# Decoder layer with RWKV-7 heads: b and k are brought to the recurrence as rows of tokens

## What is computed

```python
def rwkv7_recurrence(r, w, k, v, a, b):
    def step(state, inp):
        r_t, w_t, k_t, v_t, a_t, b_t = inp
        sa = jnp.einsum('bhvk,bhk->bhv', state, a_t)
        state = (state * w_t[:, :, None, :] + sa[..., None] * b_t[:, :, None, :]
                 + v_t[..., None] * k_t[:, :, None, :])
        y_t = jnp.einsum('bhvk,bhk->bhv', state, r_t)
        return state, y_t
    ...
def rwkv7_group(u, ...):
    u = u + f(mu_shift) * (token_shift(u) - u)
    r, k, v, wl, al, gl = jnp.split(u, RWKV_SPLITS, axis=-1)
    ...
    y = rwkv7_recurrence(r_h, hs(decay), k_mod, v_h, -kk, kk * alpha_h)

def reference(x, ...):
    h = rms_norm(x, pre_mix_norm[layer])
    proj = (h @ w_in[layer]).astype(jnp.float32)
    y_rwkv = rwkv7_group(proj[..., :RWKV_COLS], ...)
    y_pool = multiscale_pool(proj[..., RWKV_COLS:], ...)
    mixed = jnp.concatenate([y_rwkv, y_pool], axis=-1) @ w_out[layer]
    x = x + rms_norm(mixed, post_mix_norm[layer])
    f = conv_ffn(rms_norm(x, pre_ffn_norm[layer]), w_up, conv_w, conv_b, w_down)
    x = x + rms_norm(f, post_ffn_norm[layer])
```

## Time and profile before

| | us |
|---|---|
| median of three runs | 2341.03 |
| lowest, highest | 2337.63, 2349.45 |
| the profiled execution's own time | 2339.92 |
| its span on the core | 2338.1 |
| project phase | 0 to 549 |
| recurrence | 549 to about 850 |
| busy TensorE, VectorE, ScalarE, GpSimd | 2232.0, 1760.7, 1142.7, 1016.1 |

### The profile page before, as it was taken

One profiled execution on the slowest core, in us unless ns is written; L12 is line 12 of the kernel. 1 busy time (PEld: TensorE's weight loads), 2 busy tenths in 40 slices (PEclk: granted clock), 3 DMA queues, 4 the chain that ended last, 5 costly groups with the idle time before them and its releaser, 6 DMA issues.

```text
span 2338.1 us, 43613 instructions
## 1 busy us (share of the span) xinstructions
PE 2232.0 (95%) x16652; PEld 1816.3 (78%) x16652; DVE 1760.7 (75%) x1905; ACT 1142.7 (49%) x1794; POOL 1016.1 (43%) x726
## 2 busy tenths in 40 slices
PE   7999999996989979998999999999999999999998
PEld 5787777775878758886888888788788888887886
DVE  2666798894785466768999998666799898986555
ACT  4656555452445554444444444454544444444543
POOL 4646465571233335534777767100146555541000
PEclk9999999998999989999999999999999999999999
DMA  7374556347567547886434343677743233326774
GB/s 197 96 234 128 191 148 208 105 143 211 150 171 190 143 135 235 268 279 177 148 110 151 108 149 122 218 248 250 245 129 115 93 111 105 112 94 209 239 259 145
DMA packets 435786, 395.60 MB, mean 169 GB/s; under 512 B 59516, under 2 KB 352044, under 8 KB 432300
## 3 DMA queue, kind: packets, MB, share of 16 engines
q1 hardware_dynamic: 407772, 343.06, 47.6%
q10 hardware_dynamic: 27856, 50.34, 6.0%
HBM read 266.97 MB, written 126.35 MB: 168 GB/s over the span
## 4 chain that ended last, share of the span: by engine, by line
PE 54%; DVE 3%; DMA 2%; ACT 1%; issue 1%; SPq 1%; POOL 0%; ACTq 0%; DVEq 0%; POOLq 0%
PE late_bank L133 18%; PE late_bank L135 18%; PE late_bank L134 18%; DVE wt_lo L2886 1%; DMA raw<-scratch_td 1%; ACT wt_hi L2707 1%; PE late_bank L2181 1%; DMA raw<-in_w_up 0%; DMA raw<-in_w_down 0%; DVE wt_lo L2840 0%; DMA p_keep<-in_w_down 0%; DMA p_keep<-scratch_td 0%; DVE conv_val L2867 0%; DVE p_ub L2849 0%; SPq L1966 0%
## 5 line engine op out<-in xcount | busy, mean ns | idle before, releaser
L133 PE MATMUL late_bank<-o_hi,wt_hi 128*128 128x512 f32 x1232 | 482.1, 391 | 9.6 <-DVE p_ub L2849 3.1
L134 PE MATMUL late_bank<-o_lo,wt_hi 128*128 128x512 f32 x1232 | 481.4, 391 | 0.0
L135 PE MATMUL late_bank<-o_hi,wt_lo 128*128 128x512 f32 x1232 | 481.2, 391 | 0.0
L426 POOL TENSOR_TENSOR p_w_lo<-p_w_raw,p_w_hi 128x1024 fp32r<-128x1024 f32 x72 | 190.4, 2645 | 217.3 <-ACT p_w_hi L494 217.3
L133 PEld LDWEIGHTS late_bank<-o_hi,wt_hi 128*128 128x128 f32 x1232 | 232.3, 189 | 60.9 <-issue 9.5
L135 PEld LDWEIGHTS late_bank<-o_hi,wt_lo 128*128 128x128 f32 x1232 | 232.5, 189 | 48.6
L134 PEld LDWEIGHTS late_bank<-o_lo,wt_hi 128*128 128x128 f32 x1232 | 232.3, 189 | 48.2
L2577 POOL TENSOR_TENSOR tsum<-raw 128x512 f32<-128x512 f32 x43 | 104.1, 2420 | 366.0 <-DVE p_ub L2927 180.7
L133 PE MATMUL p_ppr<-p_hT_hi,p_w_hi 128*128 128x512 f32 x576 | 233.3, 405 | 0.3 <-POOL p_w_lo L426 0.2
L133 PE MATMUL late_bank<-wt_hi 128*128 128x512 f32 x572 | 223.2, 390 | 7.7 <-ACT wt_hi L2707 6.0
L135 PE MATMUL p_ppr<-p_hT_hi,p_w_lo 128*128 128x512 f32 x576 | 226.5, 393 | 0.0
(11 more groups left out here) (327 smaller groups left out, 4669.2 us busy)
## 6 DMA issues: line engine op xcount, KB each, us to landing
raw<-in_w_up SPq DMA_DIRECT2D x88, 512.0 KB, 5.1
p_w_raw<-in_w_in SPq DMA_DIRECT2D x72, 512.0 KB, 3.9
scratch_a<-p_keep SPq DMA_DIRECT2D x22, 1280.0 KB, 4.5
raw<-scratch_a SPq DMA_DIRECT2D x96, 256.0 KB, 3.0
raw<-scratch_td SPq DMA_DIRECT2D x52, 256.0 KB, 3.5
p_keep<-scratch_a SPq DMA_DIRECT2D x47, 256.0 KB, 3.0
scratch_a<-p_keep SPq DMA_DIRECT2D x44, 256.0 KB, 2.0
raw<-in_w_down SPq DMA_DIRECT2D x44, 256.0 KB, 4.1
```

What stands on the lines that cost most here:

```text
L133: nc.tensor.matmul(out, lhs_hi, rhs_hi, start=start, stop=False, skip_group_check=again)
L134: nc.tensor.matmul(out, lhs_hi, rhs_lo, start=False, stop=False, skip_group_check=again)
L135: return nc.tensor.matmul(out, lhs_lo, rhs_hi, start=False, stop=stop, skip_group_check=again)
L426: nc.gpsimd.tensor_tensor(w_lo[i][:, :, :], w_raw[i][:, :, :], w_hi[i][:, :, :].bitcast(F32), ALU.subtract).then_inc(s_wl, 1)
```

## The change

In the project phase b and k are turned into rows like v and a: `turn_b` at pair 8 (in the last block ahead of its last tile), k of the block before at pair 1 (for the last block at the very end). ScalarE reads both (`b_rows` behind the last tile of a block, `k_rows` at f = 3 of the next) and stores them as "bT" and "kT", 1 MB each for a block, and several waits are moved to them. In the recurrence `bkt` has another layout and is zeroed once by GpSimd; SyncE loads its rows from "bT" and "kT", eight loads of 32 partitions x 2 x 256 for a superchunk (`load_rows`). The transposes of `bk` and ScalarE's reads of them go; GpSimd still builds `bk` for the Gram products. TensorE's order is another: `w_products` stand behind the first `from_state`, `z0_products` behind the second, the Gram products are spread over the last two chunks. ScalarE's reads of w move to the front.

The core of the diff:

```diff
@@ phase_project, scalar
+                def b_rows(b):
+                    act.wait_ge(s_btn, ONE + b + 1)
+                    act.wait_ge(s_vst, ONE + b * 16 + 16)
+                    read_rows(gate, [pm[:, g, :] for g in range(TT)], s_br)
+                    act.wait_ge(s_br, ONE + b + 1)
+                    store_rows("bT", b, gate[:, :, :], s_brst)
...
+                        if f == 3 and b > 0:
+                            k_rows(b - 1)
...
+                        if f == (FT - 1 if more else FT - 2):
+                            b_rows(b)
...
+                k_rows(BLOCKS - 1)
@@ phase_project, gpsimd
                     if f == K0:
                         gp.wait_ge(s_kst, ONE + b * 16)
+                        gp.wait_ge(s_ktn, ONE + b)
@@ phase_project, tensor
+                    if b < BLOCKS - 1:
+                        pe.wait_ge(s_br, ONE + b + 1)
                     for g in groups:
...
+                    if pair == 1 and b > 0:
+                        pe.wait_ge(s_ar, ONE + b)
+                        pe.wait_ge(s_kt, ONE + b)
+                        rows(um[:, K0:K0 + PAIRS, :], [pm[:, g, :] for g in range(TT)], s_ktn)
+                    if pair == 8 and b < BLOCKS - 1:
+                        turn_b(b)
...
+                            if b == BLOCKS - 1 and f == FT - 1:
+
+
+                                turn_b(b)
                             for k in range(KT):
+                                if b == BLOCKS - 1 and f == FT - 1 and k == 1:
+                                    pe.wait_ge(s_br, ONE + b + 1)
...
+                pe.wait_ge(s_pout, ONE + BLOCKS * 2)
+                pe.wait_ge(s_kt, ONE + BLOCKS)
+                rows(um[:, K0:K0 + PAIRS, :], [pm[:, g, :] for g in range(TT)], s_ktn)
@@ phase_recur, sync
+                def load_rows(n):
+                    if n < 2:
+                        sp.wait_ge(s_const, ONE + 3)
+                    else:
+                        sp.wait_ge(s_s, ONE + (n - 1) * CH)
+                    for e in range(2):
+                        for kind in range(2):
+                            for h in range(2):
+                                dst = bkt[n % 2][quad(kind, h), :, h, :, :].rearrange("s (c e) j v -> s e c (j v)", e=2)[:, e]
+                                sp.dma_start(dst, bkrow[(kind + e) % 2][n, e, h]).then_inc(s_rows[n % 2], 16)
...
+                    if a2 and i >= 0:
+                        load_rows(i + 1)
@@ phase_recur, gpsimd
-                        if b:
-                            wait_full(gp, i - 1, "bk3")
+                        if i >= 0:
+                            gp.wait_ge(s_gram, ONE + i + 1)
@@ phase_recur, tensor
+                        if c4 == 0:
+                            pe.wait_ge(s_rows[p], ONE + i // 2 * 128 + 128)
...
                     if a2:
-                        bk_transposes(0)
+                        w_products()
...
                     if a2:
-                        bk_transposes(1)
+                        z0_products()
                     if b:
                         to_state(1)
                     if o:
                         from_uv()
-                    if a2:
-                        bk_transposes(2)
                     if b:
                         from_state(2)
-                    if a2:
-                        bk_transposes(3)
+                    if o:
+                        from_r(1)
                     if b:
                         to_state(2)
-                    if o:
-                        from_r(1)
-                    if a2:
-                        z0_products()
+                    if a1:
+                        grams(0)
                     if b:
                         from_state(3)
                     if a1:
-                        grams(0)
+                        grams(1)
                     if b:
                         to_state(3)
-                    if a2:
-                        w_products()
                     if a1:
-                        for j in range(1, PAIRS):
+                        for j in range(2, PAIRS):
                             grams(j)
```

## The result

| | us |
|---|---|
| median of four runs after | 2380.6 |
| lowest, highest | 2377.5, 2381.7 |
| before, beside it (four runs) | 2340.4 |
| ratio after / before | 1.0163, 95% interval 1.0134 to 1.0192 |
| the profiled execution's own time, its span | 2380.6, 2378.8 |

Slower by 40 us, where 17 were forecast: the time lies above the range. In the two traces the recurrence's first load is issued at 549.3 before and at 571.3 after; the first `to_state` of body 15 lies at 822.3 and 860.9. So the project phase costs 22 us, as forecast, the recurrence up to body 15 another 16.5 us, where 4 were to be gained, and the rest some 2.

The account below looks back on a forecast made before the run. TensorE was taken to bound the project phase and SyncE's issue time to become the recurrence's bound. 2339.9 + 22 (project phase) - 4 (recurrence: 7 gained, 3 lost to couplings) = 2358 us, range 2335 to 2370.

Parts of the forecast that it names:

- Project phase, +22: Project phase: turning b and k adds 5.0 + 7.9 + 4.4 + 4.7 = 22 us, bounds 16 and 27.
- TensorE's body of 13.2 us: Recurrence: without the four transpose groups (2.4 us) TensorE alone could do a body in 13.2 us, from 15.35.
- The 0.2 us a body of new stalls in the chain: Recurrence: the new product order adds about 0.2 us of stalls between state products and updates, 13.0 becoming 13.2.
- A set of row loads, 4.6 us of SyncE: Recurrence: eight added 64 KB loads a body take 4.1 to 5.3 us of SyncE's issue time, 4.6 taken.
- SyncE as the bound: Recurrence: with the row loads SyncE needs 16.9 us a body, against the 13.2 that TensorE could do.
- All of SyncE's 53 us of waits can be used: Recurrence: 74 us of added issue fill SyncE's 53.1 us of waits, so its last loads end at 812, not 791.3.
- The couplings, 3 us: Recurrence: late inverse block and late bonus and gate loads together lose 3 us, cutting the gain from 7 to 4.
- the other coupling: Recurrence, body 4: the last inverse block's load comes some 8 us later, delaying VectorE's solving step before the first state update.
- Rival 3: Recurrence: TensorE's stalls lower its clock, 10 to 12 us longer, 2370; chance 0.12 with anything above 2366.
- My own sign for it: Recurrence: TensorE's clock falling under 0.9 between bodies 8 and 14 would show the forecast wrong the other way.
- Rival 1: Recurrence: the loads are hidden, bodies run at TensorE's or VectorE's pace, 30 us gained, 2332; chance 0.12.
- the 7 us gained at SyncE's pace: Recurrence: with all SyncE waits used, body 15 begins at 815 instead of 822.3, 7 us gained before the couplings.

## Why the prediction was wrong

- **Project phase, +22.** Right: 22.1 us in the trace of after, 22.5 in the run of this half alone. Its parts are less exact, and that they cancel is luck: the first dense product of the fourth block comes 14.3 us later than in before (415.67 for 401.40), where three seams and two turns of k gave 11.2; the fourth block adds 3.8 more up to its last dense product (552.94 for 534.86), for 6.1; and the end adds 4.0, for 4.7.
- **TensorE's body of 13.2 us.** Right as a lower bound (12.99 in body 8 of after), wrong as a pace: without row loads the bodies at full clock mostly take 14 to 15, and 7 of 15 run at a lower one. The 0.2 us a body of new stalls in the chain were too few: TensorE's waits for VectorE's updates grow by 14.4 us in sum there (7.0 to 21.4), and stops for instructions were not in the sum at all.
- **A set of row loads, 4.6 us of SyncE.** Right: 72.4 us for 128 loads, 4.5 a set. SyncE as the bound is right too: no loads, half of the loads and the shared loads show it.
- **All of SyncE's 53 us of waits can be used.** Wrong by 11: 11.4 us of waits remain, 4.9 of them for the place of a row set itself. The last gate load of bodies with loads, at 790.55 in the earlier trace rows, comes at 839.34, 26.7 us later beyond the project's 22.1, where 74 - 53 = 21 were reckoned.
- **The couplings, 3 us.** This is the step that failed. I had the chain (gate, GpSimd, mix store) and its 3.6 us of slack, but let only the second update wait behind it. I even wrote that TensorE stands there 2 to 4 us in most bodies, and then put 3 us for both couplings into the sum, as if SyncE's pace would hide the rest; no row showed that it would. It does not: bodies 4 to 13 of after take 18.8 us in the mean, where SyncE's pace was to be 16.9. The new order puts the w reads behind that same store, and `TURN` puts y into w0's bank, so that TensorE stands already at the y transposes, ahead of the second product with the state, for up to 7.8 us and 25.8 us in sum. Reordering did not cure it: with the w reads ahead the wait went to u, with gate ahead to VectorE and GpSimd. With SyncE's queue full something else was late in each order tried, and the price is paid in body after body, not once at the end. The late inverse block, the other coupling, came 11.5 us late instead of 8 (load at 666.44; 632.79 + 22.1 = 654.9 expected without the change), in the same body 4 in which gate was late too; the runs with one of the two moved show that either alone keeps that body at 24 us or more.
- **The start.** Not reckoned: the first `to_state` comes 5 us later than with the project half alone, behind eight more loads and the w products, which wait for inverse blocks. The one attempt to undo it failed, so how the 5 us divide is not shown.
- **Rival 3, the clock.** It is there: bodies 4 to 13 of after have a mean of 14.66 us of TensorE busy time at clocks down to 0.73, against 12.93 at full clock. It comes behind the waits and adds to them; I had it as a case of its own with 10 to 12 us, and did not join it to the forecast, although I forecast waits of 2 to 4 us in most bodies, and a stand of 2.5 us brought it on (body 12 above). My own sign for it, a clock under 0.9 between bodies 8 and 14, came true with 0.77 in body 9.
- **Rival 1, loads hidden.** Even with no loads its 2332 is not reached: 2361. The 26 us that the shorter TensorE body should give, had nothing else been late, were 5.
- **The terms, by the runs.** Project half +22.5; recurrence without row loads 5 less, +17.3; its row loads +22.9; together the +40.2 of after. So the project term and SyncE as the place of the loss were seen rightly; what the loads cost, and what the missing transposes give, were not.

In the forecast's own sum: +22 held; the 7 us gained at SyncE's pace shrink to 1 (26.7 for 21); and the couplings, with the start and the clock behind the waits, are the rest of the 16.5, some 18 us instead of 3; how much of it is couplings, start and clock each is known only as far as the bodies above tell.

## What to carry to other kernels

Before work is moved from a compute engine to loads, add up the issue time of the queue for each body, not its waits over the whole. When that sum nears the body's length, the last loads of the queue come late in body after body, and each costs as much as what waits for it; the orders tried here only moved the loss. Keep the added loads under the slack, or share them between two issuing queues; here four on each did what eight on one did not. And a gap that a removed product leaves between serial steps gives back only a part of its length: put the work back in a harmless form and see how much time it costs before counting on it. Where a matmul engine stops without a releaser, look whether a packet of its instruction queue landed just before it went on.

## What the runs showed of the hardware

- A long stand of TensorE brought its clock down, and the products behind it were slower. In the stand of 7.79 us in body 4 of after the granted clock falls from 1.00 to 0.50 and is 0.50 until 676; the eight products with the state behind it take 1.11 us and the 32 of z0 1.97, against 0.68 and 1.15 at 2.4 GHz. A stop of 2.53 us did the same in the run without row loads (1.00 ahead of it, 0.50 from 799.9 to 809).

```profile
669.26 1.09 PE L1828 MATMUL late_bank<-p_ident,p_y 128*128 128x128 f32 x4 [7.79 <-ACT p_w L1450]
671.91 1.11 PE L1721 MATMUL late_bank<-p_st,w 128*64 128x64 f32 x8 [1.56 <-DVE p_st L1601]
672.95 1.97 PE L1776 MATMUL late_bank<-p_uv,am 64*64 64x64 f32 x32
```

- TensorE stops for up to 3 us in the midst of independent products, with no releaser in the profile, and goes on 1.2 to 1.7 us after a 16 KB packet of the instruction queue has ended (110 of 110 stops over 0.5 us). In sum: 6.5 us between 590 and 870 in before, 3.9 in after, 10.8 without row loads, 22.6 when 96 short matmuls a body are added, 5.2 when 16 long ones are added instead.
- A DMA of 64 KB holds SyncE's queue for 0.43 us in the median and 0.52 in the mean of the 128 row loads of after (0.57 with the step to the next), one of 256 KB for 0.52 to 0.63 where nothing stretches it; the small ones land 2.1 to 3.3 us after their issue in the median, gate (256 KB, last in the body) 5.5.
